# Context attention inside the heads stage, and bias rows written by GpSimd memsets instead of eight on-chip DMAs

## The reference, cut to what matters

```python
q = rms_norm(q.reshape(b, t, N_Q_HEADS, HEAD_DIM), q_gain)      # 12 query heads of 64
k = rms_norm(k.reshape(b, t, N_KV_HEADS, HEAD_DIM), k_gain)     # 4 key/value heads
...
def attend(q, k, v):
    s = jnp.einsum('bqhgd,bkhd->bhgqk', q, k) * (HEAD_DIM ** -0.5)
    p = jax.nn.softmax(s, axis=-1)
    return jnp.einsum('bhgqk,bkhd->bqhgd', p, v)
...
a_ctx = attend(qc.reshape(b, t, N_KV_HEADS, Q_PER_KV, HEAD_DIM), kc, vc)   # 256 queries x 256 keys
y_lat = merge(blocked_attention(ql, k_all, v_all), ...)                    # 2048 queries x 2304 keys
```

## Time and profile before

| | us |
|---|---|
| median of 3 runs | 3764.25 (3763.88 to 3771.09) |
| the profiled execution's own time | 3764.65 |
| its span, first to last instruction | 3763.0 |
| first instruction of `heads` on its queue | 605.3 |
| first instruction of the context attention | 708.06 |
| first instruction of the latent attention | 758.64 |

### The profile page before, as it was taken

One profiled execution on the slowest core, in us unless ns is written; L12 is line 12 of the kernel. 1 busy time (PEld: TensorE's weight loads), 2 busy tenths in 40 slices (PEclk: granted clock), 3 DMA queues, 4 the chain that ended last, 5 costly groups with the idle time before them and its releaser, 6 DMA issues. The chain is left out here.

```text
span 3763.0 us, 51601 instructions
## 1 busy us (share of the span) xinstructions
PE 3458.2 (92%) x16932; PEld 2598.2 (69%) x16932; DVE 2302.2 (61%) x3529; ACT 1339.1 (36%) x2250; POOL 1824.3 (48%) x1267
## 2 busy tenths in 40 slices
PE   6999996789999999999949979989999998999798
PEld 4787884356666666666548869878778786887586
DVE  4666544566666666666536664266575644777576
ACT  2432333424444444444420023233444422664200
POOL 1133313447777777777723333423486612445364
PEclk8999998789999999999979989999999999999899
DMA  5234536511111111111145445564545446777563
GB/s 187 98 107 129 148 99 202 168 36 35 40 36 34 34 35 34 34 34 34 25 156 198 169 152 180 189 198 145 184 126 176 139 152 193 215 222 245 192 215 137
DMA packets 361638, 482.64 MB, mean 128 GB/s; under 512 B 86780, under 2 KB 212876, under 8 KB 361312
## 3 DMA queue, kind: packets, MB, share of 16 engines
q1 hardware_dynamic: 296048, 345.40, 29.8%
q10 hardware_dynamic: 54256, 97.73, 8.6%
q0 software_dynamic: 11136, 36.98, 2.5%
HBM read 339.81 MB, written 137.72 MB: 127 GB/s over the span
## 5 line engine op out<-in xcount | busy, mean ns | idle before, releaser
L2132 DVE TENSOR_REDUCE al_mx<-al_sx 128x1 f32<-128x512 f32 (+1 forms) x960 | 562.4, 632 | 268.0 <-PE al_sx L2209 254.8
L2072 ACT ACTIVATE al_e<-al_st 128x1024 f32<-128x1024 f32 x432 | 443.0, 1026 | 576.8 <-PE al_st L2222 567.3
L2102 POOL TENSOR_TENSOR al_acc_p<-al_acc_p,al_e 128x1024 f32<-128x1024 f32 x192 | 457.5, 2383 | 20.0 <-POOL al_acc_p L2098 0.4
L235 PE MATMUL pb_acc<-p_whi,pb_r_hi 128*128 128x512 f32 x952 | 379.8, 399 | 39.5 <-DVE pb_r_lo L1606 29.8
L2231 PE MATMUL al_acc<-al_e,vres 128*64 128x512 f32 x1728 | 402.5, 601 | 0.0
L236 PE MATMUL pb_acc<-p_wlo,pb_r_hi 128*128 128x512 f32 x952 | 376.5, 395 | 0.0
L237 PE MATMUL pb_acc<-p_whi,pb_r_lo 128*128 128x512 f32 x952 | 376.4, 395 | 0.0
L1606 DVE TENSOR_TENSOR pb_r_lo<-pb_stg,pb_r_hi 128x512 fp32r<-128x512 f32 x238 | 248.0, 1045 | 167.1 <-ACT pb_r_hi L1504 162.8
L2221 PE MATMUL al_st<-al_qa,kres 128*128 128x512 f32 x864 | 344.8, 399 | 3.7 <-DMA al_qb<-al_negm 3.3
L2222 PE MATMUL al_st<-al_qb,kres 128*128 128x512 f32 x864 | 340.4, 394 | 0.0
L2098 POOL TENSOR_TENSOR al_acc_p<-al_e 128x1024 f32<-128x1024 f32 x48 | 160.4, 3341 | 306.4 <-ACT al_e L2072 306.4
(11 more groups left out here) (325 smaller groups left out, 7321.7 us busy)
## 6 DMA issues: line engine op xcount, KB each, us to landing
pb_stg<-s_hsum ACTq DMA_DIRECT2D x238, 256.0 KB, 2.8
s_proj<-pj_stage SPq DMA_DIRECT2D x90, 256.0 KB, 2.1
s_proj<-pb_out SPq DMA_DIRECT2D x72, 256.0 KB, 3.0
p_wst<-in_w1s ACTq DMA_DIRECT2D x18, 1024.0 KB, 6.2
ml_k<-s_proj SPq DMA_DIRECT2D x36, 512.0 KB, 4.3
ml_v<-s_proj SPq DMA_DIRECT2D x36, 512.0 KB, 8.8
mo_in<-s_proj SPq DMA_DIRECT2D x34, 512.0 KB, 6.3
hm_w<-in_ada_w SPq DMA_DIRECT2D x16, 1024.0 KB, 9.1
```

Of the source, the lines that this page charges most:

```text
L235: nc.tensor.matmul(out, s_hi, m_hi, start=start, stop=False)
L2072: nc.scalar.activation(e[:, pair(p, j), :, :], st[(NP * p + j) % 2][:, :, 0:W], ACT.Exp).then_inc(e_done, 1)
L2102: nc.gpsimd.tensor_tensor(acc_p[:], acc_p[:], e[:, pair(p, j)], ALU.add).then_inc(add_p, 1)
L2132: V.tensor_reduce(mx[:, x:x + 1], slots[x % NSX][:, 0:spans[x % NS][1]], AX.X, ALU.max).then_inc(sx_max, 1)
```

## The change

The stage of its own for context attention goes, with its barrier. A class `ContextAttention` holds the same steps, and each engine's loop over the 18 tiles calls them with a lag: in iteration n the PE computes `folded` of unit n - 7, `scores` of n - 5 and `values` of n - 6 between the transposes and the modulation product, and `high_scores` of n - 2 at the iteration's end. DVE has `bias` (one reduction over both query tiles, where two and a small third stood) with lag 3, `norm` with 7, `sums` with 6; ACT `exponentials` with 5 and `out` with 6; POOL `row` with 3 and `store` with 8. After the 18 tiles a few more iterations finish the last units (END = 19). The queries come in four groups of three heads, in DMAs that SP issues early in the loop; the results are stored from POOL. `folded` and `high_scores` share one PSUM tile (`sx`), with waits for that. The eight DMAs and the two DVE memsets for the bias rows go; in its iterations 0 to 3 POOL writes them by four memsets each over 1152 columns (zeros over 64 partitions, then ones in one partition, for both halves of a block).

```diff
+class ContextAttention:
+    def __init__(self, nc, m, a, s, kres, vres):
...
+        self.qa, self.qb = m.sb("ca_qa", [P, NQ, W], F32R), m.sb("ca_qb", [P, NQ, W], F32R)
+        self.negm = m.sb("ca_negm", [P, NQ, CT], F32R)
+        self.sx, self.st, self.res = m.ps("ca_sx", (P, CT, W)), m.ps("ca_st", (P, CT, W)), m.ps("ca_res")
+        self.fo = self.sx[:, 0, 0:CT * (HD + 1)].rearrange("p (s d) -> p s d", s=CT)
...
+    def load(self, sp, g):
+        mine = slice(QPK * g, QPK * (g + 1))
+        if g == 0:
+            sp.dma_start(self.fold[:], self.a["fold"]).then_inc(self.fold_ld, 16)
+        sp.dma_start(self.qa[:, mine, :].bitcast(F32), self.s["q"][mine, :, 0:self.W].rearrange("h p n -> p h n")).then_inc(self.q_ld[g], 16)
+        sp.dma_start(self.qb[0:HD, mine, :].bitcast(F32), self.s["q"][mine, 0:HD, 0:self.W].rearrange("h p n -> p h n")).then_inc(self.q_ld[g], 16)
+    def constants(self, dve):
+        self.nc.vector.memset(self.qb[HD:P].bitcast(F32), 0.0).then_inc(self.fixed, 1)
+        self.nc.vector.memset(self.ones[:], 1.0).then_inc(self.fixed, 1)
+    def high_scores(self, pe, n):
+        pe.wait_ge(self.q_ld[n // QPK], 32)
+        if n:
+            pe.wait_ge(self.negm_done, n)
+        if n >= 5:
+            pe.wait_ge(self.o_done, n - 4)
+        for i in range(CT):
+            x = self.nc.tensor.matmul(self.sx[:, i, :], self.qa[:, n, i * P:(i + 1) * P], self.kres[:, n // QPK, 0:self.W], start=True, stop=True)
+        x.then_inc(self.sx_mm, 1)
+    def bias(self, dve, n):
+        dve.wait_ge(self.sx_mm, n + 1)
+        self.nc.vector.tensor_reduce(self.negm[:, n, :], self.sx[:], AX.X, ALU.max, negate=True).then_inc(self.negm_done, 1)
+    def row(self, pool, n):
+        pool.wait_ge(self.negm_done, n + 1)
+        if n == 0:
+            pool.wait_ge(self.fixed, 1)
+        for i in range(CT):
+            pool.dma_start(self.qb[HD:HD + 1, n, i * P:(i + 1) * P].bitcast(F32), self.negm[:, n, i:i + 1].bitcast(F32)).then_inc(self.row_ld[n], 16)
+    def scores(self, pe, n):
+        g = n // QPK
+        pe.wait_ge(self.row_ld[n], 16 * CT)
+        if n:
+            pe.wait_ge(self.e_done, n)
+        for t in range(CT):
+            keys = slice(t * P, (t + 1) * P)
+            self.nc.tensor.matmul(self.st[:, t, :], self.kres[:, g, keys], self.qa[:, n, :], start=True, stop=False)
+            x = self.nc.tensor.matmul(self.st[:, t, :], self.kres[:, NKV + g, keys], self.qb[:, n, :], start=False, stop=True)
+        x.then_inc(self.st_mm, 1)
+    def exponentials(self, act, n):
+        act.wait_ge(self.st_mm, n + 1)
+        if n >= 2:
+            act.wait_ge(self.pv_mm, n - 1)
+            act.wait_ge(self.asum_done, n - 1)
+        self.nc.scalar.activation(self.e[:, n % 2], self.st[:], ACT.Exp).then_inc(self.e_done, 1)
+    def values(self, pe, n):
+        pe.wait_ge(self.e_done, n + 1)
+        if n:
+            pe.wait_ge(self.ot_done, n)
+        for t in range(CT):
+            x = self.nc.tensor.matmul(self.res[t * HD:(t + 1) * HD, 0:self.W], self.vres[:, t, n // QPK, :], self.e[:, n % 2, t, :], start=True, stop=True)
+        x.then_inc(self.pv_mm, 1)
+    def sums(self, dve, n):
+        dve.wait_ge(self.e_done, n + 1)
+        if n >= 2:
+            dve.wait_ge(self.fold_mm, n - 1)
+        self.nc.vector.tensor_tensor(self.asum[:, n % 2, :], self.e[:, n % 2, 0, :], self.e[:, n % 2, 1, :], ALU.add).then_inc(self.asum_done, 1)
+    def out(self, act, n):
+        act.wait_ge(self.pv_mm, n + 1)
+        if n >= 2:
+            act.wait_ge(self.fold_mm, n - 1)
+        self.nc.scalar.activation(self.ot[:, n % 2, :], self.res[:, 0:self.W], ACT.Copy).then_inc(self.ot_done, 1)
+    def folded(self, pe, n):
+        if n == 0:
+            pe.wait_ge(self.fold_ld, 16)
+            pe.wait_ge(self.fixed, 2)
+        else:
+            pe.wait_ge(self.o_done, n)
+        pe.wait_ge(self.negm_done, min(n + 5, NQ))
+        pe.wait_ge(self.ot_done, n + 1)
+        pe.wait_ge(self.asum_done, n + 1)
+        for i in range(CT):
+            cols = slice(i * P, (i + 1) * P)
+            self.nc.tensor.matmul(self.fo[:, i, 0:HD], self.ot[:, n % 2, cols], self.fold[:, 0:HD], start=True, stop=True)
+            x = self.nc.tensor.matmul(self.fo[:, i, HD:HD + 1], self.asum[:, n % 2, cols], self.ones[:], start=True, stop=True)
+        x.then_inc(self.fold_mm, 1)
+    def norm(self, dve, n):
+        dve.wait_ge(self.fold_mm, n + 1)
+        self.nc.vector.reciprocal(self.rden[:, n % 2, :], self.fo[:, :, HD]).then_inc(self.rden_done, 1)
+        dve.wait_ge(self.rden_done, n + 1)
+        self.nc.vector.tensor_tensor(self.o[:, n], self.fo[:, :, 0:HD], self.rden[:, n % 2, :].unsqueeze(2).broadcast_to([P, CT, HD]), ALU.mult).then_inc(self.o_done, 1)
+    def store(self, pool, n):
+        pool.wait_ge(self.o_done, n + 1)
+        pool.dma_start(self.s["attn"][0:self.W, n * HD:(n + 1) * HD].rearrange("(t p) d -> p t d", p=P), self.o[:, n]).then_inc(self.stored, 16)
+    def all_stored(self, pool):
+        pool.wait_ge(self.stored, 16 * NQ)
...
-    rows = m.sb("hd_rows", [P, T // 2], F32R)
...
+    ca = ContextAttention(nc, m, a, s, kres, vres)
+    END = NQ + 7
+
+    def blocks(eng, n, *steps):
+        for step, lag in steps:
+            if 0 <= n - lag < NQ:
+                step(eng, n - lag)
...
+            ca.load(sp, 0)
             for n in range(NT):
+                if 0 < n < NKV:
+                    ca.load(sp, n)
...
-                if n == 4:
-                    sp.wait_ge(rows_done, 2)
-                    for h in range(NKV):
-                        for i in range(2):
-                            sp.dma_start(kres[HD:P, NKV + h, i * (T // 2):(i + 1) * (T // 2)].bitcast(F32), rows[0:HD].bitcast(F32)).then_inc(row_ld, 16)
-            sp.wait_ge(row_ld, 32 * NKV)
...
+                blocks(act, n, (ca.exponentials, 5), (ca.out, 6))
...
+            for n in range(NT, END):
+                blocks(act, n, (ca.exponentials, 5), (ca.out, 6))
...
+            def bias_rows(h, i):
+                x = kres[:, NKV + h, i * (T // 2):(i + 1) * (T // 2)].bitcast(F32)
+                if h or i:
+                    pool.wait_ge(rows_done, 2 * h + i)
+                nc.gpsimd.memset(x[HD:P], 0.0).then_inc(rows_zero, 1)
+                pool.wait_ge(rows_zero, 2 * h + i + 1)
+                nc.gpsimd.memset(x[HD:HD + 1], 1.0).then_inc(rows_done, 1)
...
+                if n < NKV:
+                    pool.wait_ge(table_done, n + 2)
+                    pool.wait_ge(rs_done, n + 2)
+                    for i in range(2):
+                        bias_rows(n, i)
+                    pool.wait_ge(rows_done, 2 * n + 2)
+                blocks(pool, n, (ca.row, 3), (ca.store, 8))
+            for n in range(NT, END + 1):
+                blocks(pool, n, (ca.row, 3), (ca.store, 8))
+            ca.all_stored(pool)
...
-            V.memset(rows[:].bitcast(F32), 0.0).then_inc(rows_done, 1)
-            dve.wait_ge(rows_done, 1)
-            V.memset(rows[0:1].bitcast(F32), 1.0).then_inc(rows_done, 1)
...
+            ca.constants(dve)
             for n in range(NT):
                 if n:
                     products(n)
                     turned(n)
                 scaled(n)
+                blocks(dve, n, (ca.bias, 3))
                 normal(n)
+                blocks(dve, n, (ca.norm, 7))
                 if n:
                     low_part(n - 1)
+                blocks(dve, n, (ca.sums, 6))
             low_part(NT - 1)
+            for n in range(NT, END):
+                blocks(dve, n, (ca.norm, 7), (ca.sums, 6))
             mod.spread(dve, keep, 1)
...
+                if n == 5:
+                    pe.wait_ge(rows_done, 2 * NKV)
+                blocks(pe, n, (ca.folded, 7), (ca.scores, 5), (ca.values, 6))
                 if n == 0:
                     pe.wait_ge(mod.const, 32)
                 if n < PIECES:
                     mod.products(pe, n)
                 if n >= 2 and n % 2 == 0:
                     mod.fold(pe, n // 2 - 1)
+                if n == 2:
+                    pe.wait_ge(khi_done, CT)
+                blocks(pe, n, (ca.high_scores, 2))
+            for n in range(NT, END):
...
-    attention(nc, m, a, s, keep, kres, vres, "ac_", 0, CT, 1, CT)
-    m.end()
     attention(nc, m, a, s, keep, kres, vres, "al_", CT, 4, LT // 4, NT)
```

More of the change, by code:

```diff
@@ L1721, in tile @@
         fn(n + step, q, w)
+class ContextAttention:
+    def __init__(self, nc, m, a, s, kres, vres):
+        self.nc, self.a, self.s, self.kres, self.vres = nc, a, s, kres, vres
+        self.W = W = CT * P
+        self.qa, self.qb = m.sb("ca_qa", [P, NQ, W], F32R), m.sb("ca_qb", [P, NQ, W], F32R)
+        self.negm = m.sb("ca_negm", [P, NQ, CT], F32R)
+        self.e, self.asum, self.ot = m.sb("ca_e", [P, 2, CT, W]), m.sb("ca_asum", [P, 2, W]), m.sb("ca_ot", [P, 2, W])
+        self.rden, self.o = m.sb("ca_rden", [P, 2, CT]), m.sb("ca_o", [P, NQ, CT, HD])
```

(11 more changed lines are left out.)

## The result

| | before | changed |
|---|---|---|
| median of 6 runs | 3764.96 us | 3745.82 us |
| lowest to highest | 3763.75 to 3771.34 | 3742.72 to 3753.2 |
| the profiled execution, and its span | 3764.65, 3763.0 | 3744.45, 3742.7 |
| mean granted clock of that execution | 0.954 | 0.957 |
| heads' first DMA to the latent attention's | 153.3 us | 138.1 us |

The ratio is 0.995, with a 95% interval of 0.9934 to 0.9966: faster by 19 us where 26 were forecast, inside the range. The last line of the table (605.3 to 758.6 before, 603.7 to 741.8 now) is what the experiments are compared by; I call it the *stretch*. Of the 20.2 us between the two profiled executions it holds 15.2. The rest, 1.6 us ahead of the stretch and 3.4 behind it, lies in stages whose instructions are the same in both.

What follows compares the result with a forecast made beforehand. It took `heads` as bound by DMA for most of its length, with a separate 50.6 us context stage behind; 63 us saved less 38 given back gained 25.4, from 3764.65 to 3739 us, range 3720 to 3762.

Steps and rivals of the forecast that it cites:

- Memsets: Iterations 0 to 3: sixteen wide memsets on POOL at 1.1 us each, making 8.1 us per iteration.
- The rival of dear memsets: Iterations 0 to 3: each POOL memset takes 3.76 us, 42.6 us more in all, time 3782; chance 0.07.
- The gap: Between tiles 8 and 9 of `heads`: the eight bias row DMAs cost about 12.6 us, which the change removes.
- Start of the steady state: PE enters iteration 5 at about 655.4; iterations 5 to 7 take 6.2 us each, ending at 674.
- Iterations 8 to 15: Three engines need about 5 us each; with handovers 5.6, with low clock stretches 6.0 us per iteration, ending at 722.
- 0.4 more for stretches at the low clock: Iterations 8 to 15: 0.4 us added to the 5.6 of each iteration for half-clock stretches, giving 6.0.
- The rival that the clock stays low all through: Iterations 8 to 15: TensorE keeps 1.2 GHz, 9.4 us each, 27 more in all, 3766, no change; chance 0.08.
- signs of being right: In the changed profile, among others: spacing of 5.5 to 6.5 us in iterations 8 to 15, clock 0.8 or more.
- Tail: Iterations 16 and 17 take 4.2 and 2.5 us, then 1.3 to the last store's issue, at 730.0.
- The boundary: End of the merged stage: 3.2 us from the last store's issue to the next stage's first DMA, at 733.2.
- 63 us less 38: Whole change: context stage's 50.6 and 12.6 us of DMA delay go, 38 given back, about 20 to memsets; 25.4 gained.
- ACT idle ahead of the exponentials: Steady iterations: a sign of being wrong, with POOL waiting for ACT's squares; that loop, some 9 us per two iterations, counted as covered.

Runs made afterwards that it cites:

- the second trace: The changed kernel measured once more without any edit, for the spread of the traces: stretch 135.3 us, median 3744.93 us, ratio 0.9948 to the kernel before.

## Why the prediction came out as it did

The time came inside the range, and the part between `heads` and the latent attention shows how much of that was luck. In it 25.4 us were to be gained and 15.2 were; another 5 of the 20.2 us between the two profiled executions lie in stages that the change leaves as they are, and the steady state begins 3.8 us sooner than forecast, which hides part of what the later steps lacked. By its own steps, on the clock of the changed trace:

- *Memsets*: 1.1 us forecast, 1.05 measured; `scaled` of tiles 1 to 5 came 7.9, 7.8, 8.2 and 8.8 us apart where 8.1 was forecast. The rule of the Trainium skill beside it (GPSIMD Engine Reference, Elementwise — side-by-side cycle accounting) gave 0.99, a little under what was measured. The rival of dear memsets falls.
- *The gap*: gone, as the experiment with the memsets alone shows by itself. (The reading that DVE, ACT and POOL were each busy for 70 to 80% beside it was a little high: in the first window of the earlier trace rows ACT and POOL are at 66%.)
- *Start of the steady state*: forecast 674, the transposes of tile 8 at 670.23. Of these 3.8 us, 1.6 are the earlier start of the stage and 0.8 PE's entry into iteration 5, at 653.02 instead of 655.4; the other 1.4 is that iterations 5 to 7 took 5.7 us each, not 6.2. No wait for `hd_rope` was over 4.8 us after 642.
- *Iterations 8 to 15*: 6.0 forecast, 6.7 measured. The timeline of PE, in a view that ends at 724 and so shows three of the last four, has the transposes of tiles 8, 9 and 16:

```profile
670.23 0.66 PE L2071 MATMUL hd_tk<-keep_ident,hd_rot 128*128 128x128 f32 x4 [1.29 <-DVE hd_rot L2022]
...
680.16 1.05 PE L2071 MATMUL hd_tk<-keep_ident,hd_rot 128*128 128x128 f32 x4
...
723.67 0.55 PE L2071 MATMUL hd_tk<-keep_ident,hd_rot 128*128 128x128 f32 x3 [1.37 <-DVE hd_rot L2022]
```

  53.4 us for eight, 5.4 too few in the sum. Tile 8 alone took 9.9 us at half clock, as the low-clock price of 9.4 had it; the full-clock tiles took 5.0 to 6.0. With "0.4 more for stretches at the low clock" the mechanism was right and the size half of what it was: the steady state ran at 0.79 (0.83 in the second trace), and one at a clock of 1.00 needed 5.9 with 1.3 us of added PE work, close to my 5.6 for work and handovers. The rival that the clock stays low all through (9.4 us) did not come; 6.7 and 0.79 lie just outside the 5.5 to 6.5 and the 0.8 or more that I had named as signs of being right.
- *Tail*: 10.0 us instead of 8.0, from the transposes of tile 16 to the last store's issue at 733.71. Iteration 16 took 4.8 us where 4.2 were counted, the rest 5.2 where 3.8 were; in it PE's last fold stood for DVE's sum, a handover that the sum put at nothing:

```profile
731.52 0.41 PE L1823 MATMUL ca_sx<-ca_fold,ca_ot 128*128 128x64 f32 x2 [1.02 <-DVE ca_asum L1804]
```

- *The boundary*: "From the last store's issue to the next stage's first DMA it was 3.2 us": this is the step that failed. It was read in the context stage before, where SP issues the stores and POOL's drain (3.07 us, at 728.6) is hidden under PE's last units:

```profile
L1999 POOLq DRAIN  x1: 3072/3072/3072, 728.6 to 728.6; - x1
```

  In the changed kernel POOL issues stores, rows and `un`, 54 software DMAs, has to wait for the last store, and drains for 4.46 us with nobody beside it: 8.1 us, 4.9 too few. The run with the stores on SP, which brings back 3.2 us in the same merged block, shows that it is this.

Together 5.4 + 2.0 + 4.9 - 3.8 = 8.5 us, the distance between the forecast 733.2 and 741.78.

What the sum hid: I gave the two halves as if each had its own gain, 63 us less 38. The runs show that they aren't separable. Alone the memsets change the stretch by -0.7 us and the merge by +1.8 (-3.9 with its DMAs earlier); together by -15 to -18. My reading is that the memsets pay because the merge lets the query loads run under them, which no run tests by itself, and that the merge pays because no DMA stands between PE and its scores, which the 23.2 us of PE's wait show.

The forecast named ACT idle ahead of the exponentials, with POOL waiting for ACT's squares, as a sign against it. Both are there, 29.8 us over 10 waits and 14.9 over 9 between 640 and 742. With the transposes done twice they are still 25.6 and 12.0 between 654 and 724, at the shorter spacing of 5.9: they are not what made it 6.7, and whether they have a part in the 5.9 no run tells.

What stays open: what ends and begins the half-clock stretches in the steady state. That a denser PE got the full clock is seen in one window, in the clocks of four whole executions and in the order of the medians, not proved.

## What to carry to other kernels

When work is moved into a stage, look who issues its last DMA: on POOL the block's end waits for that DMA and then for a drain that grew with each software DMA issued in the block, on SP it does not. Before a row is made by a DMA, ask who will read it first in the new order, since a load that nothing waited for becomes a stop for an engine that is in order. And PE busy at half clock was not a bound that less work lifted here: look at the granted clock first, try what takes waits away, and compare medians of several runs, since the low stretches move from run to run.

## What the runs showed of the hardware

- POOL's DRAIN at the end of `heads` took 1.53, 3.48 and 4.46 us after 18, 42 and 54 DMAs that POOL had issued in the block, whatever their size (0.5 KB to 128 KB): 0.04 us and 0.082 for each DMA. Three later blocks of the kernel before lie on the same line: 16, 18 and 32 DMAs of 512 KB gave 1.36, 1.52 and 2.67 us. It does not hold everywhere. In three of the experiments 42, 54 and 54 DMAs gave 3.58, 4.56 and 4.56, 0.1 more. In the context stage of the kernel before 24 row DMAs gave 3.07, 1.1 more than the line; there the drain began at 728.6, while the last row was still being issued, which may be the reason and is not shown. Of the six blocks in which POOL issues no DMA, one has 0.04 us and five 1.39 to 3.24, so a drain has other parts too.
- A memset of one partition by 1152 elements took POOL as long (1051 ns) as one of 64 partitions (1054 ns), and was no slower while the DMA share was 1.07.
- About 15 us of added transposes went with a granted clock of 1.00 instead of 0.79 to 0.83 over 56 us, and did not make the kernel slower; that the one brought the other is not proved.
